# Value tiles 512 columns wide from two weight chunks at once, in a two-layer streaming encoder on one NeuronCore

## The reference

```
x = x + 0.5 * swiglu(rmsnorm(x), w_ffn1_gu, w_ffn1_down)
h = rmsnorm(x)
even: qa,ka,va,fa,qb,kb,vb = split(h @ w_in)      # 512 columns each, fa 8
      x += concat(forgetting_attention(qa,ka,va,fa), stick_breaking_attention(qb,kb,vb)) @ w_out
odd:  qc,kc,vc,qd,kd,vd = split(h @ w_in)         # kd, vd 128 columns
      x += concat(chunked_relbias_attention(qc,kc,vc), sliding_window_gqa(qd,kd,vd)) @ w_out
x = x + 0.5 * swiglu(rmsnorm(x), w_ffn2_gu, w_ffn2_down)
x = x + sigmoid(rmsnorm(x) @ w_gate) * (p[i] @ w_proj)
```

## Time and profile before

| | |
|---|---|
| median of 3 runs | 1047.08 us |
| profiled execution, its own time | 1047.2 us |
| its span, first to last instruction | 1045.5 us |
| mean granted TensorE clock | 0.997 |
| PE busy | 1030.4 us (99%) |
| DVE busy | 757.4 us (72%) |
| ACT busy | 587.9 us (56%) |
| the chain that ended last, by engine | PE 94%, DVE 4% |

### The profile page before, as it was taken

One profiled execution on the slowest core, in us unless ns is written; L12 is line 12 of the kernel. 1 busy time (PEld: TensorE's weight loads), 2 busy tenths in 40 slices (PEclk: granted clock), 3 DMA queues, 4 the chain that ended last, 5 costly groups with the idle time before them and its releaser, 6 DMA issues.

```text
span 1045.5 us, 18268 instructions
## 1 busy us (share of the span) xinstructions
PE 1030.4 (99%) x6596; PEld 921.8 (88%) x6596; DVE 757.4 (72%) x1352; ACT 587.9 (56%) x1003; POOL 51.6 (5%) x100
## 2 busy tenths in 40 slices
PE   9999999999999999999999999999999999999996
PEld 8888888998888888888998888889987888888896
DVE  5988765667658887765888787656766787886576
ACT  6666545545646665554666565445654665654463
POOL 1000001000011000000010000010000200000000
PEclk9999999999999999999999999999999999999998
DMA  9675457594315655457647654577733376545741
GB/s 318 211 234 165 143 160 212 175 299 135 116 63 189 214 171 183 132 166 231 215 143 238 196 173 139 155 208 223 241 112 102 126 239 194 189 138 147 212 148 41
DMA packets 225384, 185.52 MB, mean 177 GB/s; under 512 B 3665, under 2 KB 223537, under 8 KB 225201
## 3 DMA queue, kind: packets, MB, share of 16 engines
q1 hardware_dynamic: 222832, 180.94, 55.5%
q10 hardware_dynamic: 2496, 3.86, 1.1%
HBM read 183.59 MB, written 1.07 MB: 177 GB/s over the span
## 4 chain that ended last, share of the span: by engine, by line
PE 94%; DVE 4%; issue 1%; ACT 1%; DMA 1%; DVEq 0%; SPq 0%; ACTq 0%
PE ps L1386 42%; PE ps L1391 22%; PE ps L1317 4%; PE ps L1308 4%; PE ps L1309 4%; PE ps L1310 4%; PE ps L1318 2%; PE ps L1501 2%; PE ps L1502 2%; PE ps L1503 2%; DVE wsp L895 1%; PE ps L1577 1%; PE ps L1590 1%; PE ps L1618 1%; DVE probs L1110 1%
## 5 line engine op out<-in xcount | busy, mean ns | idle before, releaser
L895 DVE TENSOR_TENSOR wsp<-raw,wsp 128x1024 fp32r<-128x1024 f32 (+1 forms) x381 | 416.3, 1109 | 59.9 <-ACT wsp L590 59.1
L590 ACT ACTIVATE wsp<-raw 128x1024 fp32r<-128x1024 f32 (+1 forms) x381 | 354.4, 957 | 25.5 <-PE ps L1310 20.6
L1386 PE MATMUL ps<-xsA,wsp 128*128 128x512 f32 x960 | 229.0, 391 | 0.0
L1386 PEld LDWEIGHTS ps<-xsA,wsp 128*128 128x128 f32 x960 | 176.4, 188 | 34.3
L1386 PE MATMUL ps<-hff,wsp 128*128 128x512 f32 x616 | 145.0, 390 | 0.0
L1386 PEld LDWEIGHTS ps<-hff,wsp 128*128 128x128 f32 x616 | 113.8, 188 | 22.8
L1391 PEld LDWEIGHTS ps<-xsA,wsp 128*128 128x128 f32 x960 | 122.9, 191 | 4.5
L1391 PE MATMUL ps<-xsA,wsp 128*128 128x256 f32 x960 | 124.7, 283 | 0.0
L910 DVE TENSOR_TENSOR sq<-ps,sq 128x512 f32<-128x512 f32 x88 | 60.5, 688 | 87.4 <-ACT sq L606 87.0
L606 ACT ACTIVATE sq<-ps 128x512 f32<-128x512 f32 x88 | 51.9, 590 | 110.7 <-PE ps L1391 109.0
L652 ACT ACTIVATE xsA<-xT,gains 128x256 fp32r<-128x256 f32 x48 | 24.4, 507 | 135.2 <-DVE xT L1044 120.4
(11 more groups left out here) (205 smaller groups left out, 1440.5 us busy)
## 6 DMA issues: line engine op xcount, KB each, us to landing
raw<-in_w_ffn_gu_dram SPq DMA_DIRECT2D x87, 1024.0 KB, 5.1
raw<-in_w_ffn_down_dram SPq DMA_DIRECT2D x64, 704.0 KB, 4.6
raw<-in_w_in_even_dram SPq DMA_DIRECT2D x11, 1024.0 KB, 6.2
raw<-in_w_in_odd_dram SPq DMA_DIRECT2D x9, 1024.0 KB, 6.1
raw<-in_w_ple_gate_dram SPq DMA_DIRECT2D x8, 1024.0 KB, 5.8
raw<-in_w_out_even_dram SPq DMA_DIRECT2D x4, 1024.0 KB, 5.1
raw<-in_w_out_odd_dram SPq DMA_DIRECT2D x4, 1024.0 KB, 7.0
raw<-in_w_ple_proj_dram SPq DMA_DIRECT2D x2, 1024.0 KB, 4.9
```

Of the source, the lines that this page charges most:

```text
L590: act.activation(wsp[:, s, 0, half * n:(half + 1) * n], raw[:, s, half * n:(half + 1) * n], ACT.Copy).then_inc(hi, 1)
L895: dve.tensor_tensor(wsp[:, s, 1, sl], raw[:, s, sl], wsp[:, s, 0, sl].bitcast(F32), ALU.subtract).then_inc(lo, 1)
L1386: pe.matmul(ps[:, bank, :], whi, moving.rearrange("p s t -> p (s t)"), start=first and i == 0, stop=False)
```

## The change

The two value chunks of layer 0 group 1 and of layer 1 group 0 are read together. Where four tiles stood (two chunks by two blocks of 128 tokens, all 8 contraction steps, 256 columns) there are now four half-tiles: for each block of 128 tokens a "half" (contraction steps 0 to 3) and a "vv" (steps 4 to 7), with 512 columns, 256 from each of two neighbouring ring slots; both accumulate in one PSUM bank. The moving operand is a view of two slots; in layer 1 the pair is slots 3 and 0, read with a negative step. Each half-tile has 12 matmuls of 512 columns instead of 24 of 256. ACT does nothing for a "half" and copies 512 columns after a "vv". The number of tiles is unchanged. Layer 0 group 0 keeps its narrow value tiles.

Both chunks are now read by all four tiles, so `chunk_ends` and `in_units` give both free after the fourth; PE waits ahead of the first for both chunks.

```diff
+def chunks_of(tile):
+    chunk, _, what, idx, _ = tile
+    return (idx[2], idx[2] + 1) if what in ("half", "vv") else (chunk,)
...
         for what, j in order:
+            if what == "v" and layer != group:
+                if j == 0:
+                    for t in range(TOK):
+                        tiles.append((chunk, 0, "half", (group, t, chunk), 1.0))
+                        tiles.append((chunk + t, 0, "vv", (group, t, chunk), 1.0))
+                chunk += 1
+                continue
...
-            ends += [T + sum(t[0] <= r for t in tiles) for r in range(ph.chunks)]
+            ends += [T + max(n + 1 for n, t in enumerate(tiles) if r in chunks_of(t)) for r in range(ph.chunks)]
...
-            ends = n + 1 == len(tiles) or tiles[n + 1][0] > tiles[n][0]
+            ends = all(tiles[n][0] not in chunks_of(t) for t in tiles[n + 1:])
             return 2 * (ph.c0 + tiles[n][0] + RING) + ends
...
-        def in_bank(n):
+        def in_bank(layer, n):
+            if IN_TILES[layer][n][2] == "vv":
+                n -= 1
             return n % 4 if n < 8 else (n - 8) % 3
...
-                        if what == "v":
+                        if what == "vv":
+                            group, t, _ = idx
+                            start, w = GROUP_W * group, 2 * 256
+                        elif what == "v":
...
-            def token_tile(out_, t, xs, weights):
-                for k in range(KD):
+            def token_tile(out_, t, xs, weights, ks=range(KD)):
+                for k in ks:
...
-                    chunk_ready(c)
-                    reuse(bank)
-                    if what in "qk":
+                    chunk_ready(ph.c0 + chunks_of(IN_TILES[ph.layer][n])[-1])
+                    if what != "vv":
+                        reuse(bank)
+                    if what in ("half", "vv"):
+                        s, ks = (ph.c0 + idx[2]) % RING, range(KD // 2) if what == "half" else range(KD // 2, KD)
+                        pair = wsp[:, s:s + 2] if s < RING - 1 else wsp[:, ::-(RING - 1)]
+                        mm = token_tile(ps[:, bank, :].rearrange("p (c n) -> p c n", c=2), idx[1], xs,
+                                        lambda k: pair[:, :, :, k * 256:(k + 1) * 256].rearrange("p c s n -> p s c n"), ks)
+                        mm.then_inc(tile_done, 1)
+                    elif is_qk(what):
...
-                    pe.wait_ge(*last_written(layer, lambda what, idx: what == "v" and idx[:2] == (group, h // 4)))
+                    pe.wait_ge(*last_written(layer, lambda what, idx: (what == "v" and idx[:2] == (group, h // 4)) or (what == "vv" and idx[0] == group)))
```

More of the change, by code:

```diff
@@ L400, in is_v, with is_qk @@
             return what[0] == "v"
+        def is_qk(what):
+            return what in "qk"
         def written(layer, n):
@@ L406, in written @@
             v = is_v(tiles[-1][2])
-            return (v_ready if v else qk_ready), sum(is_v(t[2]) == v for t in tiles)
+            return (v_ready if v else qk_ready), sum((is_v if v else is_qk)(t[2]) for t in tiles)
         def last_written(layer, want):
@@ L715, in mixer_in @@
                         act.wait_ge(rcol_ready, norm + 1)
-                        act.activation(vN[:, t, start:start + w], ps[:, in_bank(n), 0:w], ACT.Copy,
+                        act.activation(vN[:, t, start:start + w], ps[:, in_bank(ph.layer, n), 0:w], ACT.Copy,
                                        scale=rcol[:, t:t + 1]).then_inc(v_ready, 1)
@@ L1055, in forget_gate @@
                     dve.wait_ge(*written(0, n))
-                    dve.scalar_tensor_tensor(fl[:, t], ps[:, in_bank(n), 256:W_FORGET], rcol[:, t:t + 1], bf[:], ALU.mult, ALU.add).then_inc(f_biased, 1)
+                    dve.scalar_tensor_tensor(fl[:, t], ps[:, in_bank(0, n), 256:W_FORGET], rcol[:, t:t + 1], bf[:], ALU.mult, ALU.add).then_inc(f_biased, 1)
                 dve.wait_ge(f_biased, TOK)
@@ L1065, in mixer_in @@
                         inverse_root(norm)
-                    bank = in_bank(n)
+                    bank = in_bank(ph.layer, n)
                     next_tile()
-                    if not is_v(what):
+                    if is_qk(what):
                         dst = (qT if what == "q" else kT)[:, idx, :]
@@ L1518, in mixer_in @@
                 for n, (chunk, col, what, idx, scale) in enumerate(IN_TILES[ph.layer]):
-                    bank, c = in_bank(n), ph.c0 + chunk
-                    chunk_ready(c)
-                    reuse(bank)
-                    if what in "qk":
+                    bank, c = in_bank(ph.layer, n), ph.c0 + chunk
+                    chunk_ready(ph.c0 + chunks_of(IN_TILES[ph.layer][n])[-1])
[8 more added lines that the diff above has]
+                    elif is_qk(what):
                         tile8(bank, c % RING, col, xs, KD * norm if n == 0 else None, xs_lo)
@@ L1530, in mixer_in @@
                         token_tile(ps[:, bank, 0:w], t, xs, lambda k: view[:, :, k, col:col + w]).then_inc(tile_done, 1)
-                    reader[bank] = (f_biased, idx[2] + 1) if with_forget(ph, chunk) else written(ph.layer, n)
+                    if what != "half":
+                        reader[bank] = (f_biased, idx[2] + 1) if with_forget(ph, chunk) else written(ph.layer, n)
                     if n == 0:
```

## The result

The changed kernel takes 1057.65 us (median of 4 runs, 1057.28 to 1057.84) against 1047.07 us before (4 runs, 1046.94 to 1048.47): a ratio of 1.0095, interval 1.0083 to 1.0108. It is slower, as forecast, but by 10.6 us and not by 4.0. The profiled execution took 1057.28 us, its span is 1055.6 us against 1045.5, and its mean granted clock is 0.992 against 0.997.

A forecast was written before the change was run, and what follows sets the result against it. PE was taken as the bound (94% of the chain). Delays of +2.3 and +1.7 us, the 1.04 gain already in them, added 4.0 to 1047.08: 1051.1 us, 8-in-10 range 1049.2 to 1053.5.

The forecast's parts named there:

- Bound and place: PE bounds the kernel; its new delays come in layer 0 step 12 and layer 1 step 4.
- The pace: Value half-tiles of both layers: 512-column matmuls 0.228 us apart, 0.13 us less per tile, 1.04 us gained in all.
- The rival of the slow operand: Wide value matmuls reading two slots start 0.20 us apart instead of 0.12, costing 7.7 us: 1058.8; chance 4%.
- The chain over the units: Layer 0 step 12, layer 1 step 4: three refill units together make PE 2.3 and 1.7 us late, net.
- The late units cost nothing: Rival at steps 12 and 4: bunched units cause no loss, only the pace counts: 1046.0 us; chance 9%.
- After the wait of 1.76 us it did not fall: Layer 1 step 11, before the change: the granted clock stayed up after PE's longest later wait.
- the fallen clock: Rival: the clock falls in layer 0's stall of about 2.5 us, 4 us low, 2 us lost: 1053.1; chance 8%.
- Edits at nothing: Value copies to vN, four gone and four widened, run beside PE; they and the wait for both chunks cost nothing.
- Later waits: After both places PE's waits on DVE, 1.76 us in layer 1 step 11 included, stay unchanged and absorb nothing.

The follow-up runs named there:

- Experiment 1: The kernel before, narrow value tiles kept, with only the changed kernel's late release of ring slots and placing of units: 1056.91 us, ratio 1.0086.
- experiment 2: The changed kernel with ACT's and DVE's late refill units spread over later steps: 1048.53 us, ratio 1.0011.
- experiment 5: The changed kernel with late refill units spread and layer 1's exponential table loaded early, after tile 7: 1048.09 us, ratio 1.0007.
- experiment 3: The changed kernel with layer 1's exponential table loaded on ACT after tile 7, ahead of the first half-tile: 1058.11 us, ratio 1.0101.

## Why the prediction was right in sign and wrong in size

- **Bound and place.** Right: PE is the bound, and the two places are the running sum of head 12 and `normalise(4)`.
- **The pace.** Right: 0.229 measured in layer 0, 0.231 in layer 1 (754.38 to 756.69), 0.228 taken. Two ring slots, and slots 3 and 0 by a negative step, cost next to nothing. The rival of the slow operand is out.
- **The chain over the units.** Right to a tenth: waits of 2.57 and 2.58 us, forecast "about 2.5"; PE 2.39 us late in layer 0, forecast 2.3, and 1.80 in layer 1 (2.76 less the 0.96 of the table load), forecast 1.7. Experiment 1 has them without the wide tiles, experiment 2 has the wide tiles without them. "The late units cost nothing" is out.
- **"After the wait of 1.76 us it did not fall"**, and with it 8% for the fallen clock. This step failed, and it makes 4.8 of the 6.6 us missed. One row without a fall was taken as a rule that waits of this length are safe. It is an outcome of one execution: with the same wait the clock fell in experiment 5's profile and stayed in before's. The rival had the right mechanism and the wrong size: it assumed one fall of 4 us, and there were two, 3.4 and 6.8 us low, up to 10.2 in other kernels. It also asked of layer 0 alone, though the prediction put a wait just as long in layer 1.
- The Trainium skill, "TensorE: Matmul & The Clock Gate", section "HAM oscillation", charges half of the throttled time as loss. The trace agrees roughly, with the half as an upper bound: of 10.3 us low 4.8 were lost where half is 5.1, and behind the old wait of experiment 5 1.2 of 3.4.
- **"Edits at nothing."** Failed for 1.0 us (a wait of 0.79, and 0.96 at the next mark by experiment 3). A copy that is gone was costed by its own time. It had also been what let the table load go ahead of the wait for the logits. The row was in the trace before, as the load at 745.69, and wasn't looked for.
- The Trainium skill, "ScalarE: Activation LUTs", section "What ACT_TABLE_LOAD costs", gives 1283 ns for the load and another 1380 ns for a drain. The trace agrees on the load (1.28 us) and shows no drain between it and the exponential (750.65 to 751.94).
- **Later waits.** Right: 0.32 and 1.76 unchanged, nothing given back.
- **The rest.** 4.2 for waits and pace, 4.8 for the clock, 1.0 for the load and 0.14 of start-up make the 10.1 us of the span. The median grew by 10.6, since the profiled execution is the fastest of the four after. Had the clock and the load been in the sum, it would have read 1057.

## What to carry to other kernels

Price a new wait of the engine that bounds the kernel twice: its length, and up to half of the time at the lower clock that may follow it; and take "it didn't fall here" from several executions, not from one. When a tile is made to hold more of a ring, look at what the later release does to the order on the splitting engines, and spread the refills before judging the tile. When an instruction goes away on ScalarE, look for a table load that stood behind it.

## What the runs showed of the hardware

- The clock fell to 0.50 around waits of 1.75 to 2.6 us, and stayed there for 3.4, 6.8 or 10.2 us, though PE was fully busy from the end of the wait on. In some executions it did not fall behind such a wait. It fell 1.4 us after PE's last matmul in layer 1 of experiment 1, and after the change 3.1 and 3.9 us after it, when PE was busy again. In the changed kernel 3.4 us low cost 1.6 us, and 6.8 cost 3.2.
- Filling a wait of 2.6 us with constant matmuls up to 0.3 us before its end kept the clock at 1.00.
- A pair of 256-column matmuls costs 239 ns and one of 512 columns 229 ns, a weight load ahead of each, with the 512 columns from one slot or from two.
- A table load of 1.28 us right ahead of an exponential began only when the exponential's inputs were there (3.04 us idle ahead of it). With a copy, or with the load placed by hand, ahead of the wait, it ran within ACT's idle time (745.69 before, 748.10 in experiment 3).
